# Reordering the modulation and gate chunks under the attention heads of a two-block transformer kernel

## Chip, cores and metric

The kernel runs on one core of one Trainium2 chip. The metric is the device time of the whole program in microseconds (us), here the median of three executions.

## What is computed

Two transformer blocks of two layers each, on 256 tokens of width 1024, all in float32. A layer of the first block is

```python
y = hybrid_mixer(x, ...)                    # three attentions, gated and merged
x = layer_norm(alpha * x + y, ...)
x = layer_norm(alpha * x + memory_cross_attention(x, mem, ...), ...)
x = layer_norm(alpha * x + swiglu_ffn(x, ...), ...)
```

and its mixer

```python
h = x @ w_in                                # queries, keys, values of A, B, C; a forget logit; gates g
branches = jnp.stack([y_a, y_b, y_c], axis=2)               # 8 heads each
proj = jnp.einsum('bsnw,nwd->bsnd', branches, w_branch)
gates = jax.nn.sigmoid(g.reshape(B, S, N_BRANCHES, D_MODEL) + b_gate)
merged = jnp.sum(gates * proj, axis=2)
return merged @ w_out
```

The second block needs, for each of its layers, a modulation vector `silu(c) @ ada_w + ada_b` of 6 x 1024 numbers for two conditions. It depends on nothing in the first block, so the kernel computes it under the first block's layers.

## The kernel before, in words

**Weights.** All weights are laid out beforehand in one stream of units of 128 x 1024 numbers, in the order of use (`stream`). A unit passes four engines: SyncE loads it to `raw`, ScalarE writes its high part `whi` (L897, `hi_part`), GpSimd the rest `wlo` (L404), TensorE multiplies with both. There are four slots. ScalarE may split a unit once TensorE has finished the unit four places earlier, and it runs its list of splits four units ahead of TensorE.

**Chunks.** Four units make a chunk, of 512 output columns. A *gate chunk* `(branch, half)` is a full product: 24 matmuls a unit over 256 tokens (L425 to L427 in `feature_units`), and ScalarE puts the four tiles out with the sigmoid (L963 in `gate_units`) when the last unit is done. A *modulation chunk*, a plain number, multiplies the unit with only four columns of `silu(c)`: four matmuls a unit (L543, L544). ScalarE then copies its row to `ytok` (L954), and TensorE turns the row into columns with eight small matmuls (L553, `modulation_columns`). VectorE adds the bias and frees the PSUM half (`modulation_bias`). The columns of a chunk are made after the second unit of the chunk that follows; only the columns of the last chunk stand by themselves, behind the last head.

**Heads.** The stage is a loop over 24 heads (`first_layer`; A, B and C with 8 heads each). Each engine has the same loop written out in its own function, and each executes its list strictly in order. TensorE does for head g: the scores of head g+1 (L568), `BEFORE_T[g]` weight units (one, none for the last four heads), the transposes of head g (L574 to L576), two weight units, and the values of head g (L587, L588). ScalarE does: the exponentials of head g+1 (L939), the split of one unit, the copy of the transposed probabilities of head g (L944), which the values wait for, two splits, and, after odd heads, the copy-out of a pair of heads (L948). The output of a gate or modulation chunk stands on ScalarE directly behind the split that belongs to the chunk's last unit. Where the function changes between sigmoid and exponential, a table load stands ahead of it. VectorE does the row minimum of the scores (L1392), the division (L1401) and the low part of the head output.

**Order under the heads.** `first_fill` runs through 71 units. The first three come ahead of the loop, and head 8 starts on the first unit of `LATE`, the list of eleven chunks, 44 units, that fills heads 8 to 23. The forget keys (L610, two sets of eight small matmuls) come directly before the first unit of `LATE` and after its second. `LATE` orders both the stream and the lists of all engines; chunk i of it uses PSUM half (i + 1) % 2. Behind the heads follow the six branch products.

Of the kernel before, what the change touches and what calls it, by code (L numbers as in the profile page):

```python
# [59 lines left out]
XA_BEFORE_T, XA_BEFORE_V = [1, 1, 1, 1], [2, 2, 2, 0]  # L60


LATE = (0, (0, 0), (1, 0), 1, (2, 0), (0, 1), 2, (1, 1), (2, 1), 3, 4)
ADA_XA, ADA_LN_XA, ADA_LN_FFN = (5, 6, 7), (8, 9), (10, 11)


# [18 lines left out]
def stream(v):  # L85
# [6 lines left out]
    def chunk(w, c, kn=KD, k=0, kper=2, width=CH):  # L92
        for j in range(k, k + kn, kper):
            unit(w, [(i, c) for i in range(j, j + kper)], width)
# [6 lines left out]
    for l in range(L):  # L101
# [16 lines left out]
        for j in (1, 2):  # L118
            chunk(w_in, C_COL + j * CH)
        for c in LATE:  # L120
            if isinstance(c, tuple):
# [77 lines left out]
def advance(steps, n):  # L199
    for _ in range(n):  # L200
        next(steps)


def build(nc, a, n_units, n_first, n_dve):
    with ExitStack() as ctx:
# [201 lines left out]
        def _(pe):  # L407
# [39 lines left out]
            def feature_chunk(*args, **kw):  # L447
                run(feature_units(*args, **kw))
# [101 lines left out]
            def modulation_columns(p):  # L550
                pe.wait_ge(mod_row, t.next(mod_row))
                for j in range(4):
                    mm = pe.matmul(lin[:, p, CH + 2 * j:CH + 2 * j + 2], ytok[0:4, j * P:(j + 1) * P], c1[0:4, C1["pick"]:C1["pick"] + 2],  # L553
                                   start=True, stop=True)
                mm.then_inc(mod_trans, 1)
# [50 lines left out]
            def forget_keys(part):  # L606
                pe.wait_ge(lin_free[0], t.next(lin_free[0]))
                for j in range(4):
                    h = 4 * part + j
                    mm = pe.matmul(lin_tile(0, j), ident[0:NH, h:h + 1].to_broadcast([NH, P]), zt(TMP + 3)[0:NH], start=True, stop=True)  # L610
                mm.then_inc(f_keys, 1)

            def first_fill():
# [44 lines left out]
                middle = lambda: forget_keys(1)  # L658
                for i, c in enumerate(LATE):
                    p = (i + 1) % 2  # L660
# [38 lines left out]
            def first_layer():  # L699
                feature_chunk(0, fresh=True)  # L700
                feature_chunk(1)
                fill = first_fill()
                advance(fill, 1)
                scores(0)
                advance(fill, 2)
                for g in range(HEADS):
                    if g + 1 < HEADS:
                        scores(g + 1)
                    advance(fill, BEFORE_T[g])
                    transposes(g)  # L710
                    advance(fill, BEFORE_V[g])
                    values(g)
                modulation_columns(1)
                for d in range(2):
                    for br in range(3):
                        if d == 0:
                            pe.wait_ge(y_lo_done, t.next(y_lo_done, 4))
                        feature_chunk((3 * d + br) % 2, 4, base=4 * br, src=(br_hi, br_lo))
                mixer_out()
                pe.wait_ge(inputs_ready, t.next(inputs_ready))  # L720
                keys = feature_units(0, src=(br_hi, br_lo))
                advance(keys, 1)
                layer_norm_mean()
                advance(keys, 2)
                layer_norm_var()
                advance(keys, 1)
                token_chunk(1, (br_hi, br_lo))
                feature_chunk(0, fresh=True)
                fill = memory_fill()
                advance(fill, 1)  # L730
                memory_scores(0)
                advance(fill, 1)
                for h in range(4):
                    if h < 3:
                        memory_scores(h + 1)
                    advance(fill, XA_BEFORE_T[h])
                    memory_transposes(h)
                    advance(fill, XA_BEFORE_V[h])
                    if h == 3:
                        modulation_columns(1)  # L740
                    memory_values(h)
                pe.wait_ge(lin_free[0], t.next(lin_free[0]))
                pe.wait_ge(lin_free[1], t.next(lin_free[1]))
                for k in range(4):
                    pe.wait_ge(y_lo_done, t.next(y_lo_done))
                    wide_unit(lambda j: lin_tile(j // 4, j % 4), k, 4, (br_hi, br_lo))
                norm_with_modulation()
                ffn()
                norm_with_modulation()
# [136 lines left out]
        def _(act):  # L886
# [81 lines left out]
            def first_fill():  # L968
# [60 lines left out]
                act.wait_ge(gate_bias, t.next(gate_bias))  # L1029
                for i, c in enumerate(LATE):  # L1030
                    p = (i + 1) % 2
# [258 lines left out]
        def _(dve):  # L1290
# [84 lines left out]
            def modulation_bias(l, c, p):  # L1375
                dve.wait_ge(mod_trans, t.next(mod_trans))
                rows = l * 96 + c * 8
                tt_(mods_all[:, rows:rows + 8].rearrange("p (t s) -> p t s", s=2),
                    lin[:, p, CH:CH + 8].rearrange("p (t s) -> p t s", s=2),
                    par2("ada_b", l, 4 * c, 4).unsqueeze(2).to_broadcast([P, 4, 2]), ALU.add).then_inc(lin_free[p], 1)  # L1380
# [93 lines left out]
            def first_fill(l):  # L1474
# [25 lines left out]
                middle = lambda: forget_tiles(1)  # L1500
                for i, c in enumerate(LATE):
                    yield from units(1)
# [10 lines left out]
            def first_layer(l):  # L1513
                copy(gb[:, :], par1("b_gate", l, 0, 24)).then_inc(gate_bias, 1)
                lo_parts(8)
                fill = first_fill(l)
                advance(fill, 1)
                lowest(0)
                advance(fill, 1)
                divide(0)  # L1520
                advance(fill, 1)
                for g in range(HEADS):
                    if g + 1 < HEADS:
                        lowest(g + 1)
                    advance(fill, BEFORE_T[g])
                    if g + 1 < HEADS:
                        divide(g + 1)
                    advance(fill, BEFORE_V[g])
                    if g % 2:
                        output_lo(g // 2)  # L1530
                modulation_bias(l, LATE[-1], 1)
                dve.wait_ge(gate_ready, t.next(gate_ready, 6))
                merged = zt(MERGED, 8)
                for d in range(2):
                    for br in range(3):
                        p = (3 * d + br) % 2
                        chunk_done(2)
                        gate, out = zt(GATES + 8 * br + 4 * d, 4), merged[:, half(d)]
                        tt_(out if br == 0 else zt(TMP, 4), gate, lin[:, p, :], ALU.mult).then_inc(lin_free[p], 1)
                        settle()  # L1540
                        if br:
                            i = tt_(out, out, zt(TMP, 4), ALU.add)
                            settle()
                        if br == 2:
                            settle().then_inc(x_ready, 1)
                        if d == 1 and br == 0:
                            half_lo(0, merged)
                half_lo(1, merged)
                input_lo(br_lo[:, 0:8 * T], zt(MEM, 8), br_hi[:, 0:8 * T])
                chunk_done(8)  # L1550
                for p in range(2):
                    residual(p, wide_aux(p))
                    settle().then_inc(resid_ready, 1)
                lo_parts(1)
                centre()
                lo_parts(2)
                inverse_std()
                scale(0)
                shift("ln_mix", l, 0)
                lo_parts(1)  # L1560
                scale(1)
                half_lo(0, x)
                shift("ln_mix", l, 1)
                half_lo(1, x)
                lo_parts(4)
                lo_parts(4)
                memory_heads(l)
                chunk_done(4)
                for p in range(2):
                    residual(p, lin[:, p, :]).then_inc(lin_free[p], 1)  # L1570
                    settle().then_inc(resid_ready, 1)
                norm_with_modulation(l, "ln_xa", ADA_LN_XA)
                ffn(l, False)
                for p in range(2):
                    chunk_done(1)
                    residual(p, wide_aux(p))
                    settle().then_inc(resid_ready, 1)
                norm_with_modulation(l, "ln_ffn", ADA_LN_FFN)
# [503 lines left out]
```

## Time and profile before

| | us |
|---|---|
| median of 3 executions | 3196.26 (3195.42 to 3197.53) |
| profiled execution | 3196.45 |
| its span | 3194.7 |
| TensorE matmul busy | 2909.4 (91%) |
| GpSimd busy | 2180.9 (68%) |
| ScalarE busy | 1521.2 (48%) |
| VectorE busy | 1135.5 (36%) |

The attention stage of the first layer, from the scores beside the first forget keys to the first branch product, lies at 140.66 to 291.76 us of the span; that of the second layer at 811.69 to 960.38. Shares over the whole span say little about these 300 us. The stage is read in stretches that begin and end at the same point of a head, so that two stretches with the same content can be compared.

### The profile page before, as it was taken

The numbers are of one execution on the slowest core, as the hardware profiler recorded it, in microseconds if no ns is written. First come the engines' busy times: TensorE is split into PE (matmuls) and PEld (weight loads), VectorE is DVE, ScalarE is ACT, GpSimd is POOL, SyncE is SP. The second block draws the span as 40 slices with busy tenths as digits, with TensorE's granted clock in tenths as the row PEclk, the third lists the DMA queues.
The fourth block names the chain that finished last, engine by engine and source line by source line (L and its number), as shares of the span: only waits on it lengthen the run. The fifth ranks groups of instructions, "written<-read, shape, count | busy, mean of one in ns | idle before, by whom it ended". The sixth has DMA issues, their size and how long they took to land.

```text
span 3194.7 us, 50106 instructions
## 1 busy us (share of the span) xinstructions
PE 2909.4 (91%) x21088; PEld 2664.5 (83%) x21088; DVE 1135.5 (36%) x1855; ACT 1521.2 (48%) x1951; POOL 2180.9 (68%) x912
## 2 busy tenths in 40 slices
PE   7999979989999889878998997789989988899898
PEld 7877859978779689766998996668989977789898
DVE  2412331123214221233543343255524434453343
ACT  4665454446574544433554443335544433455343
POOL 6667778876668778845676885445576865567586
PEclk9999999999999999989999998889999989899899
DMA  6445455554445545533444553433344553334354
GB/s 215 140 151 178 158 168 182 185 188 143 155 148 192 171 165 181 189 119 120 146 154 137 184 179 116 137 101 130 131 161 146 185 167 118 113 132 159 125 185 146
DMA packets 136513, 495.27 MB, mean 155 GB/s; under 512 B 15072, under 2 KB 17760, under 8 KB 135136
## 3 DMA queue, kind: packets, MB, share of 16 engines
q1 hardware_dynamic: 131904, 480.53, 45.6%
q10 hardware_dynamic: 4384, 11.54, 1.1%
q8 instruction: 166, 2.72, 0.4%
q14 instruction: 59, 0.48, 0.1%
HBM read 488.86 MB, written 3.15 MB: 154 GB/s over the span
## 4 chain that ended last, share of the span: by engine, by line
PE 79%; DVE 8%; ACT 6%; issue 2%; POOL 1%; DVEq 1%; ACTq 1%; DMA 1%; SPq 0%
PE lin L425 17%; PE lin L426 16%; PE lin L427 16%; PE aux L425 4%; PE aux L427 4%; PE aux L426 4%; DVE k_st L1737 3%; ACT whi L897 2%; PE aux L495 2%; PE lin L451 2%; PE lin L452 2%; PE lin L453 2%; POOL wlo L404 1%; PE aux L797 1%; PE aux L568 1%
## 5 line engine op out<-in xcount | busy, mean ns | idle before, releaser
L404 POOL TENSOR_TENSOR wlo<-raw,whi 128x1024 fp32r<-128x1024 f32 x908 | 2180.7, 2416 | 998.6 <-ACT whi L897 997.7
L897 ACT ACTIVATE whi<-raw 128x1024 fp32r<-128x1024 f32 x908 | 950.1, 1057 | 1145.3 <-PE lin L427 855.1
L425 PE MATMUL lin<-in_hi,whi 128*128 128x256 f32 x3968 | 1162.5, 293 | 90.2 <-issue 33.3
L426 PE MATMUL lin<-in_lo,whi 128*128 128x256 f32 x3968 | 1138.0, 287 | 0.0
L427 PE MATMUL lin<-in_hi,wlo 128*128 128x256 f32 x3968 | 1136.9, 287 | 0.0
L425 PEld LDWEIGHTS lin<-in_hi,whi 128*128 128x128 f32 x3968 | 777.6, 196 | 132.0 <-issue 92.0
L426 PEld LDWEIGHTS lin<-in_lo,whi 128*128 128x128 f32 x3968 | 777.8, 196 | 4.6 <-issue 3.8
L427 PEld LDWEIGHTS lin<-in_hi,wlo 128*128 128x128 f32 x3968 | 776.8, 196 | 0.0
L425 PE MATMUL aux<-br_hi,whi 128*128 128x256 f32 x880 | 249.3, 283 | 7.6 <-DVE br_lo L1299 7.6
L426 PE MATMUL aux<-br_lo,whi 128*128 128x256 f32 x880 | 249.0, 283 | 0.0
L427 PE MATMUL aux<-br_hi,wlo 128*128 128x256 f32 x880 | 249.0, 283 | 0.0
L425 PE MATMUL lin<-br_hi,whi 128*128 128x256 f32 x768 | 222.6, 290 | 0.0
L426 PE MATMUL lin<-br_lo,whi 128*128 128x256 f32 x768 | 218.5, 284 | 0.0
L427 PE MATMUL lin<-br_hi,wlo 128*128 128x256 f32 x768 | 218.4, 284 | 0.0
L425 PEld LDWEIGHTS aux<-br_hi,whi 128*128 128x128 f32 x880 | 168.9, 192 | 8.2 <-DVE br_lo L1299 8.2
L426 PEld LDWEIGHTS aux<-br_lo,whi 128*128 128x128 f32 x880 | 168.9, 192 | 0.0
L427 PEld LDWEIGHTS aux<-br_hi,wlo 128*128 128x128 f32 x880 | 168.9, 192 | 0.0
L1647 DVE TENSOR_SCALAR Z<-lin,par_all 128x256 f32<-128x256 f32 x132 | 62.7, 537 | 286.1 <-PE lin L427 286.1
L425 PEld LDWEIGHTS lin<-br_hi,whi 128*128 128x128 f32 x768 | 148.5, 193 | 5.3 <-issue 5.0
L426 PEld LDWEIGHTS lin<-br_lo,whi 128*128 128x128 f32 x768 | 148.7, 194 | 0.2
L1299 DVE TENSOR_TENSOR Z<-Z,lin 128x512 f32<-128x512 f32 (+1 forms) x34 | 29.8, 876 | 334.9 <-ACT Z L1124 305.6
L427 PEld LDWEIGHTS lin<-br_hi,wlo 128*128 128x128 f32 x768 | 148.5, 193 | 0.0
(229 smaller groups left out, 3643.2 us busy)
## 6 DMA issues: line engine op xcount, KB each, us to landing
raw<-in_wstream SPq DMA_DIRECT2D x908, 512.0 KB, 3.3
Z<-in_rel ACTq DMA_DIRECT2D x2, 1536.0 KB, 8.6
Z<-in_mem_t ACTq DMA_DIRECT2D x2, 1024.0 KB, 6.9
kv_store<-Z ACTq DMA_DIRECT2D x2, 1024.0 KB, 7.2
Z<-kv_store ACTq DMA_DIRECT2D x2, 1024.0 KB, 12.5
x<-in_x_t SPq DMA_DIRECT2D x1, 1024.0 KB, 4.9
Z<-in_ctx_t SPq DMA_DIRECT2D x1, 1024.0 KB, 5.0
out_x<-x SPq DMA_DIRECT2D x1, 1024.0 KB, 3.9
```

What stands on the lines that cost most here:

```text
L404: pool.tensor_tensor(wlo[s][:, :], raw[s][:, :], whi[s][:, :].bitcast(F32), ALU.subtract).then_inc(lo_pool, 1)
L425: pe.matmul(out, wh, xh, start=start, stop=False, skip_group_check=True)
L426: pe.matmul(out, wh, xl, start=False, stop=False, skip_group_check=True)
L427: return pe.matmul(out, wl, xh, start=False, stop=stop, skip_group_check=True)
L451: pe.matmul(out, xh, wh, start=start, stop=False, skip_group_check=True)
L452: pe.matmul(out, xh, wl, start=False, stop=False, skip_group_check=True)
L453: return pe.matmul(out, xl, wh, start=False, stop=stop, skip_group_check=True)
L495: mm = pe.matmul(out, ones, src[:, k * T:(k + 1) * T], start=(k == 0), stop=(k == KD - 1))
L568: mm = pe.matmul(out, q[:, tt * P:(tt + 1) * P], k[:, 0:(tt + 1) * P], start=True, stop=True)
L897: act.activation(whi[s][:, :], raw[s][:, :], ACT.Copy).then_inc(hi_ready, 1)
L1647: dve.tensor_scalar(o[c], u[c], w[c][:, 1:2], w[c][:, 3:4], ALU.mult, ALU.add)
L1737: dve.reciprocal(k_st[:, :], wide_aux(0))
```

## The change

`LATE` gets a new order: a gate chunk first, then modulation and gate chunks in turn, a gate chunk last. The modulation chunks stay in the order 0 to 4 and the gate chunks in the order they had. Since the last chunk is now a gate chunk, the separate columns and bias behind the heads go; those of modulation chunk 4 are made within the last gate chunk.

```diff
-LATE = (0, (0, 0), (1, 0), 1, (2, 0), (0, 1), 2, (1, 1), (2, 1), 3, 4)
+LATE = ((0, 0), 0, (1, 0), 1, (2, 0), 2, (0, 1), 3, (1, 1), 4, (2, 1))
@@ first_layer, TensorE
                     values(g)
-                modulation_columns(1)
                 for d in range(2):
@@ first_layer, VectorE
                         output_lo(g // 2)
-                modulation_bias(l, LATE[-1], 1)
                 dve.wait_ge(gate_ready, t.next(gate_ready, 6))
```

All modulation chunks now use PSUM half 0 and all gate chunks half 1.

## Rows read from the trace of the kernel before

**Rows 1.** Page of the profile, section 4: the chain that ended last, by engine.

```profile
PE 79%; DVE 8%; ACT 6%; issue 2%; POOL 1%; DVEq 1%; ACTq 1%; DMA 1%; SPq 0%
```

**Rows 2.** Table of stretches: length, busy time (instructions) by engine, clock, DMA.

```profile
140.66:162.24 21.58, 21.58 (x112) 14.67 (x111) 9.18 (x32) 11.13 (x20) 14.86 (x8) 0.84 0.46 147
811.69:832.40 20.71, 20.02 (x111) 13.98 (x110) 9.18 (x32) 11.02 (x20) 14.77 (x8) 0.92 0.46 153
...
183.41:203.17 19.76, 16.02 (x95) 11.53 (x94) 3.79 (x16) 14.13 (x25) 14.63 (x8) 0.91 0.50 159
203.17:224.53 21.36, 21.36 (x167) 20.05 (x166) 3.73 (x15) 13.03 (x23) 13.85 (x6) 1.00 0.46 149
224.53:245.90 21.37, 17.71 (x96) 12.50 (x95) 3.79 (x16) 14.13 (x25) 14.61 (x8) 0.84 0.45 148
...
267.45:281.72 14.27, 10.75 (x39) 5.06 (x38) 3.63 (x15) 11.33 (x22) 7.72 (x5) 0.76 0.40 129
281.72:291.76 10.04, 9.13 (x51) 5.30 (x50) 2.54 (x10) 7.60 (x15) 9.23 (x5) 1.00 0.55 188
...
853.58:874.53 20.95, 17.19 (x95) 12.41 (x95) 3.79 (x16) 14.13 (x25) 14.63 (x8) 0.84 0.47 150
...
895.90:915.71 19.81, 16.15 (x95) 11.32 (x95) 3.79 (x16) 14.13 (x25) 14.61 (x8) 0.91 0.48 158
...
937.26:950.34 13.08, 9.56 (x40) 4.29 (x39) 3.63 (x15) 11.34 (x22) 7.83 (x5) 0.87 0.35 121
```

**Rows 3.** TensorE's waits, layer 1, then layer 2: total, times, longest.

```profile
PE aux L587 <- ACT probs L944: 10.9, 3, 3.7
...
PE aux L587 <- ACT probs L944: 10.9, 3, 3.8
```

**Rows 4.** Timeline of TensorE, first layer: start, duration, instruction, [idle before <- releaser].

```profile
141.51 1.99 PE L610 MATMUL lin<-Z,c 8*128 8x256 f32 x8
...
176.70 0.36 PE L425 MATMUL lin<-in_hi,whi 128*128 128x256 f32 x1
...
179.65 0.28 PE L425 MATMUL lin<-in_hi,whi 128*128 128x256 f32 x1
...
185.34 0.48 PE L543 MATMUL lin<-whi,silc 128*4 128x512 f32 x1
...
186.35 0.40 PE L543 MATMUL lin<-whi,silc 128*4 128x512 f32 x1
...
191.19 0.80 PE L587 MATMUL aux<-probs,Z 128*64 128x256 f32 x2 [3.74 <-ACT probs L944]
...
290.79 1.05 PE L553 MATMUL lin<-c,ytok 4*128 4x2 f32 x8 [0.91 <-ACT ytok L954]
291.76 0.39 PE L425 MATMUL lin<-br_hi,whi 128*128 128x256 f32 x1
```

**Rows 5.** Timeline of ScalarE from the end of a gate chunk.

```profile
182.79 1.06 ACT L897 ACTIVATE whi<-raw 128x1024 fp32r<-128x1024 f32 x1 [1.81 <-PE lin L427]
183.86 1.28 ACT L963 ACT_TABLE_LOAD   x1
185.16 1.57 ACT L963 ACTIVATE Z<-lin,gb 128x256 f32<-128x256 f32 x4
186.84 0.38 ACT L948 ACTIVATE br_hi<-aux 128x256 fp32r<-128x256 f32 x1
...
190.57 0.47 ACT L944 ACTIVATE probs<-aux 128x384 f32<-128x384 f32 x1
```

**Rows 6.** Table of stretches around clock changes; the clock stands before the DMA share.

```profile
144.00:147.40 3.40, 3.40 (x11) 1.40 (x10) 3.23 (x11) 2.01 (x6) 1.04 (x1) 0.54 0.50 154
...
187.40:191.20 3.80, 0.06 (x2) 0.04 (x1) 1.83 (x8) 3.63 (x8) 0.46 (x1) 1.00 0.34 128
191.20:194.90 3.70, 3.70 (x11) 1.98 (x12) 0.74 (x4) 1.80 (x3) 3.70 (x2) 0.54 0.21 42
```

**Rows 7.** Timeline of GpSimd behind the third head pair of B.

```profile
190.74 11.74 POOL L404 TENSOR_TENSOR wlo<-raw,whi 128x1024 fp32r<-128x1024 f32 x5 [4.42 <-ACT whi L897]
```

## The prediction

> **What bounds the kernel now.** I read the chain that ended last first: TensorE carries 79% of it [rows 1], so a microsecond counts only if TensorE loses or gains it. The stage in question is the attention of the first block, once per layer. I cut both layers at the starts of the score matmuls of a head and read the table of stretches [rows 2]; the reader should compare stretches of like content. Then the waits of TensorE alone in the stage [rows 3], and TensorE and ScalarE side by side around one wait [rows 4, 5]. Last the granted clock [rows 6] and GpSimd [rows 7].
>
> In one head TensorE issues the next head's scores, one weight unit, this head's transposes, two weight units, this head's values (the last four heads have no unit ahead of the transposes). A gate unit keeps TensorE for 2.95 us (176.70 to 179.65), a modulation unit for 1.01 us (185.34 to 186.35), a set of modulation columns 0.97 us (290.79 to 291.76), a set of forget keys 1.99 us [rows 4]. The stretch 203.17:224.53 is two heads with six gate units at full clock, 21.36 us [rows 2]; less six times 2.95 it leaves 1.83 us for the scores, transposes and values of one head.
>
> With these prices each stretch can be split into work and loss. 183.41:203.17, 224.53:245.90, 853.58:874.53 and 895.90:915.71 each hold a whole modulation chunk that follows directly on a gate chunk, two gate units, one set of columns and two heads: 4 x 1.01 + 2 x 2.95 + 0.97 + 2 x 1.83 = 14.57 us. They took 19.76, 21.37, 20.95 and 19.81 us [rows 2], so they lose 5.2, 6.8, 6.4 and 5.2 us. 267.45:281.72 and 937.26:950.34 hold chunk 3 and two heads (7.70 us) and took 14.27 and 13.08 us: 6.6 and 5.4 us lost. The mean of the six **gate-to-modulation losses is 5.9 us**. Stretches of gates lose nothing. TensorE's reported idle in them is 10.9 us for three in either layer [rows 3], 3.6 us each; the other 2.3 us each is work at the lower clock and the latency behind it.
>
> Where the idle comes from is on ScalarE [rows 5]. At 182.60 TensorE ends the last gate unit. ScalarE splits a weight unit (1.06), loads the sigmoid table (1.28), puts out four gate tiles (to 186.73), copies out a head (0.38, from 186.84), loads the exp table, does the exponentials, splits a unit, and only then (190.57) copies the transposed probabilities for which the values wait. TensorE had one head part and three modulation units to do, 4.86 us, to about 187.5, and starts the values at 191.19 after 3.74 us idle [rows 4]. Had the three units been gates, they would have taken 8.85 us and hidden it.
>
> The clock: in the stretch with the idle it is still 1.00, the full 2.4 GHz, and in the 3.7 us behind it 0.54, which is the 1.2 GHz level for nearly all of it [rows 6].
>
> **What the change does to this sum.** The order becomes G M G M G M G M G M G in place of M G G M G G M G G M M. The same 44 units with the same instructions are done: 24 gate units, 20 modulation units, five sets of columns, each layer. Work therefore costs nothing more, and the tail's wait for the last row copy goes. What changes is how many modulation chunks have a gate chunk directly ahead: three before (chunks 1, 2 and 3), **five after**. I price each place by where in a head the gate chunk ends. Units count from the head with index 8, three a head.
>
> - Chunk 0, before: it came ahead of all gates, mixed with two sets of forget keys. 140.66:162.24 and 811.69:832.40 took 21.58 and 20.71 us [rows 2]; content 4 x 1.01 + 2 x 2.95 + 0.97 + 2 x 1.99 + 2 x 1.83 = 18.55 us; loss 3.0 and 2.2, mean 2.6 us. After, the keys lie among gate units. The stretch 144.00:147.40 runs at 0.54 [rows 6] directly behind the first set of keys, in dense work it would cost 1.6 us; it may come or not. I take 1.0 us, between 0 and 1.6. So 1.6 us gained.
> - Chunk 0, after: the gate chunk ends in the unit ahead of head 9's transposes. TensorE then has transposes (0.25) and two modulation units, 2.27 us. ScalarE goes straight from the gate output to the copy: by [rows 4, 5] that is 4.24 us after the end of the gate chunk (186.84 against 182.60), plus 0.62 us from the start of the copy to the values (190.57 to 191.19), 4.86 us. Idle: 2.6 us. The exp table is loaded behind it, under head 10, and hidden: TensorE does head part, two modulation units and a gate unit meanwhile. The lower clock behind a shorter idle isn't shown in this place; bounds are 0 and 3.2 us (6.8 less 3.6, the worst of the six). I take 1.4 us, nearer the measured 2.3 than nothing, since modulation units lie on both sides. Together 4.0 us.
> - Chunk 1: same place, same neighbours as before. 5.9 us, unchanged.
> - Chunk 2 before stood at 224.53: 5.9 us, gone. After, it starts behind a gate chunk that ends in the first unit after head 14's transposes. ScalarE's list until the copy for head 15 is the one of [rows 5] with one more split (1.06) and without the copy-out (0.4): 8.59 - 0.40 + 1.06 = 9.25 us. TensorE has four modulation units and a head part, 5.87 us. Idle 3.4 us, with 2.3 us as measured: 5.7 us.
> - Chunk 3, after: as chunk 0, in head 17: 4.0 us. Before it stood behind heads 18 and 19 together with chunk 4: one loss of 5.9 us for both.
> - Chunk 4, after: behind the gate chunk that ends head 19, in the place chunk 3 had: 5.9 us.
> - The tail before, 281.72:291.76, 10.04 us for four modulation units, two sets of columns and two heads of which one has no scores (some 8.7 us): 1.3 us lost, 0.91 of it the wait for the row copy ahead of the last columns [rows 4]. After, two heads with gate units: nothing lost. The last gate's output still makes ScalarE late by some 4 us, but the first branch product takes two units of 2.9 us before anyone needs it, and no TensorE instruction waits.
>
> Per layer before: 2.6 + 3 x 5.9 + 1.3 = 21.6 us. After: 1.0 + 4.0 + 5.9 + 5.7 + 4.0 + 5.9 + 0 = 26.5 us. The change costs 4.9 us a layer, **9.8 us in all**. One exp table load per layer falls away at the end, off TensorE's path: nothing. The moved transfers are the same number and size; SyncE's order follows the units, and GpSimd has worked ahead when it matters: 5 units without a break behind 190.74 [rows 7], 2.35 us each, while TensorE takes 2.95 us a gate unit.
>
> On the table loads the trace and a page differ. In [rows 5] the load at 183.86 takes 1.28 us and the next activation starts at 185.16, 0.02 us behind it. The Trainium skill (ScalarE: Activation LUTs, What ACT_TABLE_LOAD costs) adds a drain of about 1.38 us to each switch. By the page the three new gate outputs would each be later by that, some 6 us more on the forecast for the kernel; the row decides, and I leave it out.
>
> **Rivals.**
> - *Short waits leave the clock alone* and the forget keys cost nothing among gates. Then the places are 0, 2.6, 5.9, 3.4, 2.6, 5.9 us: 20.4 us against 21.6, a gain of 1.2 us a layer, 3194 us. It decides if the idle of chunks 0 and 3 stays at 2.6 us with a clock of 1.00 behind it. For it: those waits are shorter by a third than any of the six. Against: the clock also fell at 144.00 with no idle reported at all. The Trainium skill (TensorE: Matmul & The Clock Gate, HAM oscillation) speaks for this rival: it ties the drop to idle gaps that are long, and short ones leave the clock up. The drop behind 187.4 agrees, the one at 144.0 does not.
> - *The alternation pays*: gate units at the end of the stage and weights worked ahead hide what the last modulation pair lost. Only the tail (1.3 us) and chunk 0 (2.6 us) can be gained beyond the rival above; if chunks 0 and 3 lost less than 1 us each, the sum would be 17.2 us a layer, 9 us less for the kernel: 3188 us. It needs ScalarE to be done 1.6 us earlier than [rows 5] show.
> - *Weights come late as well.* The split of the first gate unit behind chunks 0 and 3 starts only after ScalarE's copy: 4.24 + 0.47 + 1.06 us, then 2.35 us on GpSimd, 8.3 us after the gate chunk's end with the hand-over, when TensorE wants it at 4.86 + 1.83 + 2.02 = 8.7 us. Slack 0.4 us. If it is missed by 1 to 2 us twice a layer: 3210 to 3214 us.
>
> **How the numbers follow.** The profiled execution took 3196.45 us, its span 3194.7 and 1.75 around it that I leave as it is; it lies 0.2 us above the median of 3196.26. 3196.45 + 9.8 = 3206.2, to the median 3206.0 us. Chances: this forecast with its clock terms 0.48, late weights 0.14, clock left alone 0.32, alternation pays 0.06. Bounds of the sum: low 3194, as the first rival; high, with 3.2 us of clock behind each wait, 1.6 + 5.8 + 6.8 + 6.6 + 5.8 + 6.8 = 33.4 us a layer, 3220. I give 3194 to 3217. A measurement of this kernel tells about 0.2%, 6.4 us: above 3202.7 is slower, below 3189.9 faster. Slower 0.60, same 0.34, faster 0.06.
>
> **What the new profile should show.** Five waits of the values for the copy per layer in place of three: about 2.6, 3.7, 3.4, 2.6 and 3.5 us, 15.8 us in place of 10.9. No wait for the row copy at the end. Stretches of two heads around chunks 0 and 3 that lose 4 us, and a granted clock below 0.9 in them. If the waits are there and the total isn't, the clock terms were wrong; if the waits are missing, ScalarE's order was misread; if GpSimd releases gate units, the third rival.

## The result and the profile after

The changed kernel took 3210.5 us (median of 7 executions, 3209.0 to 3219.0) beside 3197.5 us (3194.9 to 3200.4) for the kernel before in the same sessions: ratio 1.0047, 95% interval 1.0035 to 1.0058. It is slower, by 13.0 us by the medians and 15 us by the ratio. The profiled execution took 3212.0 us, its span 3210.2, 15.5 more than the span of before.

TensorE's waits in the attention stage of the first layer, then of the second, after the change (total us, times, longest); line 943 here is line 944 of before:

```profile
PE aux L587 <- ACT probs L943: 15.6, 5, 3.8
...
PE aux L587 <- ACT probs L943: 15.6, 5, 3.8
```

Against [rows 3] that is five waits of the values for ScalarE's copy in place of three. There is no other idle time. Before, the stage also had the wait for the row copy in both layers, and one for VectorE at the forget keys in the second:

```profile
PE lin L553 <- ACT ytok L954: 0.9, 1, 0.9
PE lin L610 <- DVE Z L1469: 0.7, 1, 0.7
```

The table of stretches for the whole stage of either layer, first of before, then of after (length, busy time of TensorE, its weight loads, VectorE, ScalarE, GpSimd, then granted clock):

```profile
140.66:291.76 151.10, 139.27 (x885) 109.23 (x884) 34.10 (x134) 97.43 (x172) 102.59 (x45) 0.92 0.46 151
811.69:960.38 148.69, 136.15 (x886) 107.47 (x885) 34.11 (x134) 97.33 (x172) 102.49 (x45) 0.94 0.46 153
```

```profile
140.71:299.42 158.71, 143.07 (x886) 113.06 (x885) 33.66 (x134) 92.52 (x165) 104.23 (x45) 0.90 0.44 146
...
817.11:975.58 158.47, 142.83 (x886) 112.61 (x885) 33.67 (x134) 92.49 (x165) 104.26 (x45) 0.90 0.44 147
```

The reader should take two numbers from each row. The idle time of TensorE is the length less its busy time: 11.8 and 12.5 us before, 15.6 and 15.6 after. What the clock takes is, as an estimate, the length times what the clock lacks to 1: 12.1 and 8.9 us before, 15.9 and 15.8 after. The clock is printed with two decimals, so each of these is good to 0.8 us. What is left of a stage without both is 127.2, 127.2, 127.2 and 127.0 us: the work is the same. Idle plus clock accounts for the two layers: +3.8 +3.8 in the first, where the stage grew by 7.6 us, and +3.1 +6.9 in the second, where it grew by 9.8. So 17.4 us are found in the two stages, in about 40% as waiting and 60% as slower matmuls; outside them the span is 1.9 us shorter.

Place by place, as answers to [rows 2]: the same table cut at the heads, first layer.

```profile
140.71:157.02 16.31, 16.31 (x101) 14.35 (x100) 7.36 (x24) 5.76 (x11) 7.28 (x4) 0.90 0.37 130
157.02:174.56 17.54, 15.03 (x87) 10.65 (x86) 3.72 (x15) 13.58 (x25) 12.85 (x6) 0.90 0.37 122
174.56:186.28 11.72, 11.72 (x93) 11.05 (x92) 1.72 (x8) 4.59 (x9) 8.42 (x4) 1.00 0.54 179
186.28:207.34 21.06, 17.30 (x96) 12.52 (x95) 3.79 (x16) 14.12 (x25) 14.62 (x8) 0.84 0.44 149
207.34:239.21 31.87, 28.53 (x178) 23.43 (x177) 5.86 (x24) 17.99 (x33) 20.82 (x9) 0.89 0.46 150
239.21:258.61 19.40, 16.88 (x88) 11.12 (x87) 3.72 (x15) 13.71 (x25) 14.13 (x6) 0.82 0.47 156
258.61:270.52 11.91, 11.91 (x93) 10.97 (x92) 1.72 (x8) 4.58 (x9) 7.19 (x4) 1.00 0.43 142
270.52:283.56 13.04, 9.53 (x39) 4.38 (x38) 3.63 (x15) 11.33 (x22) 7.80 (x5) 0.87 0.37 121
283.56:299.42 15.86, 15.86 (x124) 14.59 (x123) 2.14 (x9) 6.88 (x13) 11.11 (x5) 1.00 0.49 166
```

With the prediction's prices (gate unit 2.95, modulation unit 1.01, columns 0.97, keys 1.99, head part 1.83) the losses are: start 1.7, chunk 0 3.9, chunk 1 6.5, chunk 2 6.6, chunk 3 5.8, chunk 4 5.3, the three stretches without a wait 0.6 together. The second layer's stretches give 1.7, 4.0, 6.2, 6.7, 5.7, 5.4 and 0.6.

ScalarE behind the first gate chunk, in the layout that no trace of before showed (timeline):

```profile
160.91 1.06 ACT L896 ACTIVATE whi<-raw 128x1024 fp32r<-128x1024 f32 x1 [1.21 <-PE lin L427]
161.98 1.28 ACT L962 ACT_TABLE_LOAD   x1
163.28 1.57 ACT L962 ACTIVATE Z<-lin,gb 128x256 f32<-128x256 f32 x4
164.96 0.49 ACT L943 ACTIVATE probs<-aux 128x384 f32<-128x384 f32 x1
```

and TensorE's release from it, the first of the five waits; the others are 3.76, 3.34, 2.52 and 3.51 us:

```profile
165.50 0.43 PE L587 MATMUL aux<-probs,Z 128*64 128x256 f32 x1 [2.51 <-ACT probs L943]
```

The copy starts directly behind the gate output, which starts directly behind the split of the chunk's last unit.

### The profile page after: what moved, and what is told of

Same layout as the page of the kernel before. It is cut to its first block, busy times and chain, and to the rows that moved or that the text cites. A ratio compares the mean times of both kernels' runs of the same rounds, so it can differ in the third digit from the quotient of the medians.

```text
span 3210.2 us, 50104 instructions
## 1 busy us (share of the span) xinstructions
PE 2914.6 (91%) x21088; PEld 2668.2 (83%) x21088; DVE 1135.3 (35%) x1855; ACT 1518.6 (47%) x1949; POOL 2179.2 (68%) x912
## 4 chain that ended last, share of the span: by engine, by line
PE 79%; DVE 8%; ACT 6%; issue 2%; POOL 2%; DVEq 1%; ACTq 1%; DMA 1%; SPq 0%
PE lin L425 17%; PE lin L426 16%; PE lin L427 16%; PE aux L425 4%; PE aux L427 4%; PE aux L426 4%; DVE k_st L1735 3%; ACT whi L896 2%; PE aux L495 2%; POOL wlo L404 2%; PE lin L451 2%; PE lin L452 2%; PE lin L453 2%; PE aux L796 1%; PE aux L568 1%
## 5 line engine op out<-in xcount | busy, mean ns | idle before, releaser
L426 PEld LDWEIGHTS lin<-br_lo,whi 128*128 128x128 f32 x768 | 148.7, 194 | 0.3
```

The costliest lines, as they stand in the source:

```text
L426: pe.matmul(out, wh, xl, start=False, stop=False, skip_group_check=True)
```

## The experiments

**Theory W (waits).** A *place* is from here on a modulation chunk with a gate chunk directly ahead, and a *quick unit* is a modulation unit. A modulation chunk that stands directly behind a gate chunk exposes ScalarE's gate output, and each such place costs a wait and the clock behind it. **Rivals:** the cost sits in one place only, at the start with the forget keys or at the parted pair at the end; the weights (GpSimd) are the cause; or runs of quick units are bad by themselves, so that some alternation is right and only its details cost.

### The orders

Only `LATE` differs (and whether the last chunk's columns stand behind the heads).

```diff
 # one part of the change: gate chunk first
+LATE = ((0, 0), 0, (1, 0), 1, (2, 0), (0, 1), 2, (1, 1), (2, 1), 3, 4)
 # one part: gate chunk last
+LATE = (0, (0, 0), (1, 0), 1, (2, 0), (0, 1), 2, (1, 1), 3, 4, (2, 1))
 # one part: the last pair parted
+LATE = (0, (0, 0), (1, 0), 1, (2, 0), (0, 1), 2, (1, 1), 3, (2, 1), 4)
 # the opposite: two runs
+LATE = (0, 1, (0, 0), (1, 0), (2, 0), (0, 1), (1, 1), (2, 1), 2, 3, 4)
```

Gate chunk first: 

> The order before with only its first two chunks swapped: G M G M G G M G G M M, so four modulation chunks stand directly behind a gate chunk in place of three. Theory of the waits (each such place costs what ScalarE's gate output delays the copy): modulation chunk 0 leaves its old place (2.6 us lost) for the one behind the first gate chunk, which in the profile of the changed kernel loses 3.9 us, and the forget keys among gates lose 1.65; +3 us a layer, +6 us, some 3203 us. Theory of the place (the whole slowdown comes from moving the forget keys and the start of the stage): +13 us, 3211 us. Theory of the end (it comes from parting the last two modulation chunks): 0, 3197 us.

Gate chunk last: 

> The order before with the last gate chunk moved to the very end: M G G M G G M G M M G, without the columns behind the heads. Still three gate-to-modulation places. Theory of the waits: the tail's 1.3 us goes, the pair's loss of 5.5 us becomes one of some 6.6 us, since it now begins inside a head; -1 to +1 us a layer, 3195 to 3199 us. Theory that gate units under the last heads are themselves bad: +5 us or more. Theory that the end was what the change improved: -3 us or more.

Pair parted: 

> The order before with only the last modulation pair parted by a gate chunk: M G G M G G M G M G M. Four gate-to-modulation places in place of three, nothing moved at the start. Theory of the waits: one more place of 6.6 us, the last pair's 5.5 us stays with its last chunk; +6 us a layer, +12 us, 3209 us. Theory of the place: 0, 3197 us.

Two runs: 

> Modulation chunks gathered in two runs, M M G G G G G G M M M: one gate-to-modulation place in place of three, the same units. Theory of the waits: two places of 5.9 us go; the runs are longer than the lead of the weights, GpSimd needs 2.4 us a unit where TensorE has 1.0 us plus its share of a head, so 1 to 3 us come back in each run; -12 to -17 us in all, 3180 to 3185 us. Rival (the order evens out GpSimd's load, so runs are bad and the weights become the bound): twelve units in a row wait for GpSimd throughout, some 8 us a layer lost on top, 3197 us or slower, with GpSimd as the releaser of modulation units.

Measured, each against the kernel before on the same chip: gate first 3205.1 us, ratio 1.0026 (1.0013 to 1.0039); gate last 3197.6, 1.0007 (0.9997 to 1.0018); pair parted 3210.8, 1.0050 (1.0035 to 1.0065); two runs 3179.6, 0.9954 (0.9939 to 0.9970). Two of the three parts of the change slow the kernel, the third does nothing clear of noise, and the two that do are those that add a gate-to-modulation place. By the medians the parts add up to more than the whole, since their profiled spans are 3 to 5 us longer outside the stages; in the stages they add up: 6.2, 1.9 and 9.1 us against 17.4 for the changed kernel. That the cost sits at the start alone, or at the end alone, is out: both edits cost, in different parts of the stage. The opposite edit takes two places away and wins 17 us. TensorE's waits in the first layer with the pair parted, then with two runs:

```profile
PE aux L587 <- ACT probs L944: 14.3, 4, 3.8
```

```profile
PE aux L587 <- ACT probs L944: 3.3, 1, 3.3
PE lin L553 <- ACT ytok L954: 1.3, 2, 0.9
PE lin L610 <- DVE Z L1469: 0.7, 1, 0.7
```

In these two, in the kernels before and after, and in gate first and gate last, the number of waits for the copy is the number of places, and with two runs no wait for GpSimd is in the list, so the rival fell. What the two runs still pay is the clock: behind their one wait, which ends at 256.90, TensorE works through the quick units at 0.61 in 257.00:260.50 and at 0.50 up to 271.00, and that costs some 7 us a layer, twice the wait.

Two more orders share the same run of twenty quick units. They differ in one gate-to-modulation place, and besides in the forget keys and the tail:

```diff
+LATE = (0, 1, 2, 3, 4, (0, 0), (1, 0), (2, 0), (0, 1), (1, 1), (2, 1))   # modulations first
+LATE = ((0, 0), (1, 0), (2, 0), (0, 1), (1, 1), (2, 1), 0, 1, 2, 3, 4)   # gates first
```

Modulations first: 

> All five modulation chunks first, then the six gate chunks: no modulation chunk stands behind a gate chunk. Theory of the waits: only the start's 2.6 us a layer and what twenty quick units in a row lose to the weights are left; by GpSimd's 2.4 us a unit that is 48 us of weights against some 40 us of TensorE's work with 7 us worked ahead, 1 to 5 us; stage 132 to 137 us a layer, kernel 3160 to 3170 us, faster than all others. Rival (long runs of quick units are bad in themselves, heads without cover): as slow as two runs or slower, 3180 us or more.

Gates first: 

> All gate chunks first, then all modulation chunks: one gate-to-modulation place and the tail, the same run of twenty quick units. Theory of the waits: the kernel with the modulations first plus one place (3.8 us of idle and 2 to 3 of clock) plus the tail's 1.3 us less 1 us at the forget keys, 6 to 7 us a layer: 12 to 15 us slower than it, 3174 to 3184 us. Rival (only the length of runs counts): the same as with the modulations first.

Measured: modulations first 3170.1 us (3169.6 to 3173.2), ratio 0.9930 (0.9907 to 0.9952), **faster than both kernels**; gates first 3180.9, 0.9960 (0.9945 to 0.9975). The distance is 11 us; theory W said 12 to 15, the rival 0. The time of modulations first lies at the upper edge of what was expected. Gates first has one place but three waits for the copy in the first layer, 3.66, 0.30 and 1.98 us, and 3.66, 0.30 and 1.16 us in the second: only the first of each is the place. The last two lie inside the run of quick units, where two of ScalarE's splits also wait 1.55 and 1.09 us for the load of their weights (first layer); what made them was not looked for. So the distance isn't the price of the place alone. The stages of modulations first, and its waits in the first layer:

```profile
140.74:277.53 136.79, 131.64 (x885) 104.52 (x885) 33.33 (x134) 92.36 (x165) 104.11 (x45) 0.99 0.50 169
798.34:935.74 137.40, 131.59 (x885) 104.53 (x884) 33.32 (x134) 92.20 (x165) 104.09 (x45) 0.99 0.51 168
```

```profile
PE lin L543 <- POOL wlo L404: 2.1, 3, 1.2
PE aux L587 <- ACT probs L943: 1.3, 2, 0.8
PE lin L425 <- POOL wlo L404: 1.2, 1, 1.2
PE lin L553 <- ACT ytok L953: 0.6, 1, 0.6
```

Here GpSimd does appear as the releaser, 3.3 us a layer; it is busy without a break for fifteen units:

```profile
155.20 35.08 POOL L404 TENSOR_TENSOR wlo<-raw,whi 128x1024 fp32r<-128x1024 f32 x15 [1.23 <-ACT whi L896]
```

So a long run of quick units does cost weights, as a rival had it, but 3 us where one gate-to-modulation place costs 4 to 7. The waits are short (1.2 us at most) and spread, and the clock is 0.99 over the stage; its only fall in either layer is one behind forget keys.

### The gate output

The sigmoid of the gate output is replaced by an exponential, in both kernels, so that no table load stands in the stage. These kernels leave the sigmoid out, and their gates hold other numbers; only their time is used.

```diff
-i = act.activation(..., lin_tile(p, j), ACT.Sigmoid, bias=gb[:, b:b + 1])
+i = act.activation(..., lin_tile(p, j), ACT.Exp, bias=gb[:, b:b + 1])
```

Changed kernel: 

> The changed kernel with the gate output's sigmoid replaced by an exponential, so that ScalarE needs no table load before or after a gate output (the gates then hold other numbers: this leaves the sigmoid out, nothing else). Gate outputs are 1.28 us shorter before the copy where the chunk ends ahead of the transposes, 2.56 us elsewhere. Theory of the waits: the five waits of 2.5, 3.8, 3.3, 2.5 and 3.5 us a layer become 1.2, 1.2, 0.8, 1.2 and 1.0, 10.2 us less a layer, 20 us for the kernel; with the clock no longer falling up to 18 us more: 3172 to 3190 us. Theory that ScalarE isn't the cause (weights from GpSimd, or the clock by itself): the waits change releaser and the time stays within 5 us of 3210.

Kernel before: 

> The same edit on the kernel before (sigmoid left out for an exponential). Theory of the waits: three waits of 3.6 us a layer become some 1.1, 7.5 us less a layer, 15 us for the kernel and up to 14 more by the clock: 3168 to 3182 us, and the distance between the two orders shrinks from 13 us to 1 to 6 us. If the order itself cost something else (forget keys, weights, the tail), the distance stays near 13 us.

Measured: changed kernel 3173.4 us (3172.3 to 3174.6), kernel before 3179.5 (3173.8 to 3186.6). What made the waits was ScalarE's gate output: with the table loads gone they shrink from 2.51, 3.76, 3.34, 2.52 and 3.51 us to 1.09, 2.19, 0.49, 1.09 and 1.95, the releaser stays the same, and by the ratios the changed kernel gains 36 us, the kernel before 14. The order of the two is turned round, by 6 us in the medians of four executions each (ratios 0.9933, 0.9917 to 0.9950, and 0.9955, 0.9937 to 0.9972) and by 5.3 us in the stages. I had not expected that; I had left at least 1 us of the distance. Waits of the changed kernel without loads, then of the kernel before without loads, and the stage of each in the first layer:

```profile
PE aux L587 <- ACT probs L943: 6.8, 5, 2.2
```

```profile
PE aux L587 <- ACT probs L944: 6.2, 3, 2.2
PE lin L553 <- ACT ytok L954: 0.9, 1, 0.9
```

```profile
140.89:281.81 140.92, 134.11 (x885) 107.58 (x885) 33.50 (x134) 78.76 (x155) 104.20 (x45) 0.96 0.50 165
```

```profile
140.65:284.17 143.52, 136.38 (x885) 107.53 (x884) 34.09 (x134) 81.36 (x160) 102.60 (x45) 0.94 0.49 158
```

Idle is alike, 6.8 and 7.1 us; the clock differs, 5.6 us lost against 8.6. The changed kernel's waits include three of 1.1 us and less, and behind these the clock stays in both layers, while behind those of 2.19 and 1.95 us it falls. That is no sharp rule: in the first layer of the kernel before without loads the clock stays at 1.00 behind a wait of 2.19 us that ends at 189.60, in the second it falls behind the same wait. And 1.7 of the 3.0 us of difference in the first layer lie behind the forget keys, where that kernel's clock falls twice. The table of stretches on and behind a wait of 1.09 us, then on and behind one of 2.19 us, changed kernel without loads:

```profile
161.00:164.20 3.20, 2.18 (x11) 0.74 (x9) 0.00 (x0) 2.99 (x7) 1.97 (x1) 1.00 0.51 164
164.20:168.00 3.80, 3.73 (x20) 2.22 (x21) 1.07 (x5) 2.63 (x7) 3.16 (x3) 1.00 0.41 138
187.00:189.70 2.70, 0.51 (x4) 0.06 (x2) 0.91 (x3) 2.53 (x7) 0.48 (x1) 0.99 0.58 194
189.70:193.50 3.80, 3.80 (x12) 2.10 (x13) 0.70 (x4) 1.71 (x2) 3.80 (x2) 0.56 0.24 74
```

Alternation as such, then, isn't what costs. Its five places cost because each exposes a gate output that ends about 4 us after the chunk. Why the order turned round, beyond the clock's share, stays open.

### The copy ahead of the output

Nothing is left out; ScalarE does the gate output behind its next copy of transposed probabilities (and behind the loop, what is left).

```diff
 def gate_units(p, br, d):
     yield from units(3)
     hi_part()
-    units_done()
-    for j in range(4): ...Sigmoid...
+    held.append((p, br, d, n[0]))
 def transposed(n):
     act.activation(probs_tr[:, 0:n], aux[:, 2, 0:n], ACT.Copy).then_inc(pt_ready, 1)
+    gates_held()          # waits for the chunk's last unit, then the four sigmoids
```

On the changed kernel: 

> The changed kernel with each gate output put behind ScalarE's next copy of transposed probabilities, nothing left out. Theory of the waits: the five waits go, except that gate chunks all use one PSUM half and the one that starts behind chunk 2 may wait up to 1.5 us for it; -15 us of idle a layer and most of the clock's 9 us: 3165 to 3185 us. Rival (the output only moves and delays something else by as much: the splits behind it, hence the weights): 3200 us or more, with GpSimd as releaser.

On the kernel before: 

> The same edit on the kernel before. Theory of the waits: the three waits of 3.6 us a layer go, and the clock stays up there: 5 to 6 us a place, 15 to 17 a layer, 3164 to 3175 us, faster than both kernels; the two orders then differ by less than 8 us. Rival as for the changed kernel: 3190 us or more.

On the two runs: 

> The two runs M M G G G G G G M M M with each gate output behind ScalarE's next copy. Theory that the output only moves its delay when the head behind has no gate unit either, as the wait of 3.8 us in head 21 showed: the 3.35 us ahead of head 19's values goes and about as much appears one head later, 3176 to 3182 us against 3179.6 without the edit. Rival (the copy-first order removes it): 3167 to 3172 us.

Measured: changed kernel 3192.4 us, kernel before 3182.3, two runs 3176.8 (ratios 0.9990, 0.9958, 0.9952). By the ratios the edit wins 18 and 13 us over the first two orders without it, less than the 25 us and the 22 us or more that were expected. For the two runs the times don't show a gain: 0.9952 (0.9936 to 0.9967) with it, 0.9954 (0.9939 to 0.9970) without it. Their time lies where the theory of the moved delay put it. Waits of the changed kernel with the copy first, then of the kernel before with it, first layer:

```profile
PE lin L425 <- POOL wlo L404: 4.9, 3, 2.2
PE aux L587 <- ACT probs L944: 4.7, 4, 3.8
PE lin L425 <- ACT Z L970: 1.2, 1, 1.2
```

```profile
PE aux L587 <- ACT probs L945: 5.4, 4, 3.8
PE lin L425 <- POOL wlo L404: 1.4, 2, 0.8
```

The rival that I had named came true in part. The output that is put off delays ScalarE's splits, and the gate units behind the modulation chunk wait for their weights: 2.2, 0.6 and 2.1 us in the changed order, against 0.6 and 0.8 in the old one. The wait of 1.2 us for L970 is the one for the shared PSUM half, forecast at up to 1.5. And in the last heads, which have no unit ahead of the transposes, the delay moves one head on. ScalarE there, kernel before with the copy first, and the values that waited:

```profile
260.83 0.49 ACT L945 ACTIVATE probs<-aux 128x384 f32<-128x384 f32 x1
261.34 1.28 ACT L971 ACT_TABLE_LOAD   x1
262.63 1.57 ACT L971 ACTIVATE Z<-lin,gb 128x256 f32<-128x256 f32 x4
264.37 2.00 ACT L898 ACTIVATE whi<-raw 128x1024 fp32r<-128x1024 f32 x2 [0.17 <-issue]
266.39 1.28 ACT L940 ACT_TABLE_LOAD   x1
...
268.70 0.49 ACT L945 ACTIVATE probs<-aux 128x384 f32<-128x384 f32 x1
```

```profile
269.25 0.69 PE L587 MATMUL aux<-probs,Z 128*64 128x256 f32 x1 [3.77 <-ACT probs L945]
```

The copy at 260.83 was early, the one at 268.70 late by as much as the old one. In the two runs the wait of 3.3 us became 2.1, 0.7, 0.6 and 0.2 us, together as long; their stages were still shorter in the profiled execution, 137.7 and 139.7 us against 142.1 and 142.1, since the clock was down for less time. That gain rests on one execution.

### All orders in one view

Outside the two stages the profiled spans differ by up to 13 us between kernels that are the same there (2889 to 2902 us), so the lengths of the stages say more than one span. The medians come from several sessions, in which the kernel before itself had 3197.5, 3196.9 and 3193.7 us: beside 3196.9 stand gate first, gate last, pair parted and two runs, beside 3193.7 modulations first and gates first. Each row's idle and stage are of one profiled execution.

| kernel | places a layer | idle in the stage, us | stage, layer 1 / 2, us | median, us |
|---|---|---|---|---|
| modulations first | 0 | 5.1 / 5.8 | 136.8 / 137.4 | 3170.1 |
| two runs | 1 | 5.4 / 5.3 | 142.1 / 142.1 | 3179.6 |
| gates first | 1 | 7.1 / 6.0 | 143.0 / 141.0 | 3180.9 |
| before | 3 | 11.8 / 12.5 | 151.1 / 148.7 | 3197.5 |
| gate last | 3 | 11.5 / 11.5 | 152.5 / 149.2 | 3197.6 |
| gate first | 4 | 14.3 / 14.3 | 153.8 / 152.2 | 3205.1 |
| pair parted | 4 | 15.9 / 16.2 | 153.7 / 155.2 | 3210.8 |
| changed | 5 | 15.6 / 15.6 | 158.7 / 158.5 | 3210.5 |

From none to five places the stage grows by 21.5 us, 4.3 us each; from one row to the next it is between 2 and 6. The kernel with the parted pair is as slow as the changed one with 8 us less in its stages; in its profile 7 us lie outside the stages, and what holds it there was not looked for.

## Why the prediction was right, and where it wasn't

It said slower, 3206.0 us in a range of 3194 to 3217, with 0.60 for slower by over 0.2%. Measured were 3210.5 us and a ratio of 1.0047. The way and the mechanism were right; the size was short, and part of the agreement is luck. The sum gave 9.8 us for the two stages, and they grew by 17.4 in the profiled executions; the medians are only 13.0 apart, and the profiled spans are 1.9 us closer than the stages.

- **Content equal, order counts.** Right: 885 or 886 matmul instructions in the stage in either kernel, and the stretches of gates lose nothing or 0.3 us.
- **Five places in place of three, released by ScalarE's copy.** Right in number and size: 2.6, 3.7, 3.4, 2.6 and 3.5 us forecast, 2.51, 3.76, 3.34, 2.52 and 3.51 measured; 15.8 forecast in sum, 15.6 measured. The two layouts that no row of before showed were put together from the durations of [rows 4, 5], and they hold to 0.1 us. The experiment without table loads shows the cause of the waits: they shrink with the output.
- **The tail and the forget keys.** The wait for the row copy is gone, as forecast. The keys among gates lose 1.7 us, at the upper bound of 0 to 1.6, where I took 1.0. That it may come or not was right: with the gate chunk first the same stretch loses 1.7 us in the second layer and 0.2 in the first.
- **The clock behind the waits: the term that was mis-sized.** For chunk 3 I took 1.4 us behind a wait of 2.6 us; it was 3.3 and 3.2, at the bound of 3.2. Behind the wait of chunk 2 the term was 3.3, not 2.3. Behind chunk 0 it was 1.4 to 1.5, as taken. Chunk 1 had 2.4 to 2.7 and chunk 4 1.8 to 1.9. Together a layer lost 30.4 and 30.2 us, not 26.5. The whole change was forecast at 4.9 us a layer and took 7.6 and 9.8 in the stages. In the table of stretches the clock is down longer behind chunk 3's wait than behind chunk 0's: behind the value matmuls at 247.88 the clock is down for two stretches in a row, behind those at 165.50 for one, and in 168.90:172.00 it is back at 0.89.

```profile
248.00:251.50 3.50, 3.50 (x10) 1.67 (x11) 1.02 (x4) 3.28 (x4) 2.65 (x2) 0.51 0.37 138
251.50:254.80 3.30, 3.30 (x10) 1.61 (x9) 1.05 (x5) 2.35 (x6) 2.92 (x2) 0.50 0.60 170
...
165.50:168.90 3.40, 3.40 (x11) 1.90 (x12) 1.17 (x5) 3.38 (x4) 2.43 (x2) 0.59 0.39 143
```

  Neither the chunk nor its heads are the reason. The kernel with the gate chunk first has chunk 0 in the same place, under the same heads and with the same wait of 2.51 us in both layers, and pays 2.8 us for the clock in the first and 1.5 in the second. Its stretches of chunk 0 in either layer, and the start of the stage in the first, at the full clock (table of stretches):

```profile
155.44:174.37 18.93, 16.42 (x88) 11.30 (x87) 3.73 (x15) 13.71 (x25) 13.74 (x6) 0.82 0.42 143
830.76:848.35 17.59, 15.08 (x88) 10.81 (x87) 3.72 (x15) 13.58 (x25) 12.12 (x6) 0.90 0.36 121
140.62:155.44 14.82, 14.82 (x100) 12.86 (x100) 7.37 (x24) 5.76 (x11) 7.30 (x4) 1.00 0.37 121
```

  So the 1.4 us that I took for chunk 0 and found there was luck, and so would 2.8 have been. The rows of before said it already: their six losses fall in two groups, 5.2, 5.2, 5.4 and 6.4, 6.6, 6.8 us, with nearly the same idle, and each of the three chunks is in one group in one layer and in the other in the other. I took their mean; a forecast should carry both values at each place. What decides between them was not tried.
- **The rival of short waits that leave the clock alone** fell: both waits of 2.5 us were followed by the lower clock in either layer, 0.59 and 0.51 in the first. The Trainium skill's rule (TensorE: Matmul & The Clock Gate, HAM oscillation), by which only long gaps bring the clock down, doesn't carry over to waits that lie between modulation units. The waits of 1.1 us and less in the experiment without table loads agree with it; one of 1.17 us with the copy first does not, for the clock is 0.51 in 216.40:219.80 of the first layer, and it stays up behind the same wait in the second.
- **Late weights** didn't come: there was no wait for GpSimd in the stage, so the slack, forecast at 0.4 us, was enough. With the copy first it was used up at once, 2.2 and 2.1 us in the same two places.
- **The alternation pays** was out for the kernel as it is, by the length of the gate output. Without table loads the alternation is the faster of the two, with 5.6 us lost to the clock against 8.6 for a part of it. The prediction's price for this rival was worked out wrongly in one point: the tail and the start can't be gained beyond the first rival, whose 20.4 us hold them already.
- **The table loads.** The row decided rightly: at 161.98 the load takes 1.28 us and the activation starts at 163.28. The further 1.38 us of the Trainium skill (ScalarE: Activation LUTs, What ACT_TABLE_LOAD costs) doesn't show at the gate outputs, and the waits came out at what the rows alone gave. The prediction's 6 us for it fit the two places a layer that are new in number (an estimate, 4 x 1.38 us); for the three outputs that it names it would be 8.

## What to carry to other kernels

In this kernel quick work was a poor neighbour behind a chunk whose output is long on another engine in strict order: what counted was not how evenly the quick chunks were spread, but how often one stood directly behind such an output. Gather them ahead of the first such output, as far as the weights worked ahead carry. Price each place by what the other engine still has on its list against what TensorE has until it needs it, and add the clock behind the wait with both of the values that the rows show, since the same place can take either.

## What the runs showed of the hardware

TensorE's granted clock fell to the 1.2 GHz level without any idle time reported, behind the forget keys: 0.54 in 144.00:147.40 of before, and in both layers of the changed kernel the start of the stage is at 0.90 on average with TensorE busy throughout. It doesn't always: with the gate chunk first the same stretch of the first layer is at 1.00. Each key matmul works on 8 rows (form 8*128); whether that is the reason was not tried.

Waits of 2.5 to 3.8 us ahead of the values were each followed by the lower clock in the kernels before and after. Of shorter ones some were and some were not: 1.09 us was not, 2.19 us was in three of four cases, 1.17 us in one of two. In the two stages of the changed kernel the clock cost as much as the waiting (15.9 and 15.8 against 15.6 and 15.6 us), and of what the change added to the second, 6.9 us are the clock's and 3.1 the waiting's.
